# The Fourier branch of a hybrid layer on half of its channel waves, projected as even and odd sums

## What is computed

```python
def _fourier(u):
    b, l, _ = u.shape
    uf = u.astype(jnp.float32).reshape(b, l, FNET_GROUPS, FNET_GROUP_DIM)
    y = jnp.fft.fft2(uf, axes=(1, 3), norm="ortho").real
    return y.reshape(b, l, FNET_WIDTH).astype(u.dtype)
...
    gates = jax.nn.sigmoid(h @ w_gate + b_gate).reshape(b, l, N_BRANCHES, d)
    proj = jnp.einsum("blnw,nwd->blnd", branches, w_branch)
    return jnp.sum(gates * proj, axis=2) @ w_o
```

## Time and profile before

| what | us |
|---|---|
| median of 3 runs | 1163.68 (1163.4 to 1164.49) |
| span of the profiled execution | 1160.8 |
| the rest (launch and end, by the difference from the median) | 2.9 |
| PE busy | 1093.8 (94% of the span) |
| DVE busy | 562.6 (48%) |
| ACT busy | 317.0 (27%) |
| POOL busy | 176.8 (15%) |

### The profile page before, as it was taken

How to read it: one execution, slowest core, us unless ns; L and a number is a source line. 1 busy time by engine, 2 the same in 40 slices (tenths; PEclk the granted TensorE clock), 3 DMA queues, 4 the chain that set the end, 5 groups by cost and what they waited for, 6 DMA issues and landing times.

```text
span 1160.8 us, 16298 instructions
## 1 busy us (share of the span) xinstructions
PE 1093.8 (94%) x5691; PEld 700.4 (60%) x5691; DVE 562.6 (48%) x1011; ACT 317.0 (27%) x539; POOL 176.8 (15%) x255
## 2 busy tenths in 40 slices
PE   6999999989999999999999998899999899988985
PEld 4788888868667777778888777333333233322333
DVE  5776787745676788766564546221112111111114
ACT  4542322243334544342433242100000000000003
POOL 0000110000110323345000100122222122211220
PEclk9999999999999999999999998999999999999999
DMA  9423855720111222223132489989999999999975
GB/s 380 194 97 120 293 177 194 254 91 19 55 56 55 74 73 74 91 85 130 59 109 91 179 368 343 406 352 423 423 424 425 425 426 425 426 427 426 425 321 223
DMA packets 41981, 279.68 MB, mean 241 GB/s; under 512 B 7802, under 2 KB 8186, under 8 KB 30016
## 3 DMA queue, kind: packets, MB, share of 16 engines
q1 hardware_dynamic: 34496, 265.07, 57.3%
q0 software_dynamic: 7424, 13.80, 3.4%
HBM read 274.23 MB, written 13.40 MB: 248 GB/s over the span
## 4 chain that ended last, share of the span: by engine, by line
PE 73%; DMA 14%; DVE 7%; ACT 3%; issue 2%; SPq 0%; DVEq 0%; POOL 0%; ACTq 0%; POOLq 0%
PE psum L701 70%; DMA ering<-in_wb 8%; DMA ering<-in_wa 2%; DMA ada<-in_adaw 2%; DVE ring_lo L1538 1%; PE psum L717 1%; DVE amx L1809 1%; DVE sc L1798 1%; DMA xr<-token_rows,tabt 1%; ACT ring_hi L1235 1%; PE psum L1043 1%; PE psum L741 1%; DMA Hx<-in_xT 1%; DMA gat<-expert_rows 0%; ACT gth L1235 0%
## 5 line engine op out<-in xcount | busy, mean ns | idle before, releaser
L701 PE MATMUL psum<-ering,xs 128*64 128x512 f32 x1056 | 237.0, 599 | 18.7 <-DMA ering<-in_wb 9.1
L701 PE MATMUL psum<-Hhi,ring_hi 128*128 128x512 f32 x472 | 188.3, 399 | 0.1
L701 PE MATMUL psum<-Hlo,ring_hi 128*128 128x512 f32 x472 | 185.3, 393 | 0.2 <-DVE Hlo L1538 0.2
L701 PE MATMUL psum<-Hhi,ring_lo 128*128 128x512 f32 x472 | 183.1, 390 | 0.0
L701 PEld LDWEIGHTS psum<-ering,xs 128*64 128x64 f32 x1056 | 73.2, 137 | 160.9 <-issue 135.1
L1538 DVE TENSOR_TENSOR ring_lo<-ring,ring_hi 128x1024 fp32r<-128x1024 f32 x87 | 107.8, 1239 | 109.7 <-ACT ring_hi L1235 108.6
L1538 DVE TENSOR_TENSOR sg<-sg,psum 128x256 f32<-128x256 f32 x66 | 27.8, 421 | 236.8 <-ACT sg L1235 235.6
L701 PE MATMUL psum<-ering,at 128*64 128x512 f32 x528 | 119.5, 597 | 2.9 <-ACT at L1235 1.6
L1235 ACT ACTIVATE ring_hi<-ring 128x1024 fp32r<-128x1024 f32 x87 | 92.2, 1060 | 74.3 <-DMA ring<-in_stream 41.2
L701 PEld LDWEIGHTS psum<-Hhi,ring_hi 128*128 128x128 f32 x472 | 88.7, 188 | 22.7 <-issue 3.2
L701 PEld LDWEIGHTS psum<-Hhi,ring_lo 128*128 128x128 f32 x472 | 88.5, 188 | 19.7
(11 more groups left out here) (350 smaller groups left out, 1450.7 us busy)
## 6 DMA issues: line engine op xcount, KB each, us to landing
ering<-in_w SPq DMA_DIRECT2D x28, 2048.0 KB, 21.6
ering<-in_wb SPq DMA_DIRECT2D x28, 2048.0 KB, 27.8
ering<-in_wa SPq DMA_DIRECT2D x28, 2048.0 KB, 22.8
ring<-in_stream SPq DMA_DIRECT2D x87, 512.0 KB, 4.3
ada_ring<-in_stream SPq DMA_DIRECT2D x32, 512.0 KB, 3.7
ada<-in_adaw SPq DMA_DIRECT2D x4, 2048.0 KB, 10.8
Am<-decay_rows POOLq DMA_DIRECT2D x8, 512.0 KB, 4.5
gat<-expert_rows SPq DMA_DIRECT2D x4, 1024.0 KB, 8.0
```

Source lines behind the costliest of these rows:

```text
L701: return nc.tensor.matmul(out, lhsT, rhs, start=start, stop=stop)
```

## The change

The transform of a real input is symmetric, so mixer 2 is not expanded any more to 512 waves by 512 positions.

- The channel matrix is 128 x 128: for each group 32 cosines (waves 0 to 31, wave 0 halved) and 32 sines, where the sine of wave 0, which is zero, gives its place to the alternating sum, wave 32. `V` writes one bank (0, 1, 2, 0 in turn) with 4 matmuls of 128 columns. ACT copies each `V` to one buffer that holds all four, and then the alternating columns, three times over, to `alt`, which POOL has cleared behind `("decr",)`.
- `F` are two steps of 4 x 257 and 4 x 255 columns, after all `V`. A new step `FN` transforms the alternating sums (4 matmuls of 258 columns from `alt`). ACT copies the whole of each to `fhi` and `mid`, DVE subtracts for `flo` and the low rows of `mid`.
- The projection folds the weights instead of the data. A `branch` tile of mixer 2 holds the rows of waves 0 to 31 in one half and of waves 0, 63 to 33 in the other. POOL makes their sum and difference (`mixed`, in the tile's `ring_hi` place), ACT copies that to `ring_lo` as the high half, DVE leaves the rest in `ring_hi`. POOL, ACT and DVE do this at the step that `split_at` names.
- `("proj", 2, d)` is first an odd sum over 256 positions (6 matmuls of 256 columns) into bank 0, then an even sum over 258 (6 matmuls of 258 columns, and one more of wave 32 with `mid_w`) into bank 1. ACT copies the odd sum to `odd`; DVE writes sum and difference to `mtmp` (2 operations of 255 columns, one of 2) before it multiplies by the gate.
- A further ring tile and step, `n32`, carry the weight rows of wave 32; ACT and DVE split it into `mid_w` just ahead of `("gate", 2, 0)`.
- The splits of mixer 2's output (4 on ACT, 4 on DVE) are gone. Several semaphores are merged into `step_ready`, `step_exp` and `four_ready`, with the counts in the same order.

```diff
-    t += attention() + [("V", 0), ("V", 1), ("F", 0), ("V", 2), ("F", 1), ("V", 3)] + attention()
-    t += [("F", 2), ("F", 3)] + attention() + attention()
+    t += attention() + [("V", ft) for ft in range(4)] + attention()
+    t += [("F", 0), ("F", 1), ("FN",)] + attention() + attention()
...
+        if n == 2:
+            t += [("n32",)]
...
         elif k == "V":
-            b = 5 - s[1] % 2 * 5
+            b = s[1] % 3
...
         elif k == "F":
-            b = 2 + s[1] % 2 * 5
+            b = 1 + s[1]
+        elif k == "FN":
+            b = 0
...
+        if k == "proj" and s[1] == 2:
+            used[0] = used.get(0, 0) + 1
+            plan["odd", s[2]] = (0, used[0])
...
+                if n == 2:
+
+                    b = claim(pe, ("odd", d))
+                    split_there(x)
+                    if d == 0:
+                        job_read(pe, ("FN",))
+                        pe.wait_ge(mid_w_ready, 1)
+                    for k in range(2):
+                        o = (2 + k) * 256 + d % 2 * P
+                        ins = three(bk(b)[:, 0:256], hi[:, o:o + P], lo[:, o:o + P], fhi[:, k, 256:S], flo[:, k, 256:S], k == 0, k == 1)
+                    ins.then_inc(full[b], 1)
+                    b = claim(pe, s)
+                    for k in range(2):
+                        o = k * 256 + d % 2 * P
+                        three(bk(b)[:, 0:NMID], hi[:, o:o + P], lo[:, o:o + P], fhi[:, k, 0:NMID], flo[:, k, 0:NMID], k == 0, False)
+                    mm(bk(b)[:, 0:NMID], mid_w[:, d * P:d * P + P], mid[:, :], False, True).then_inc(full[b], 1)
+                    continue
...
+            if is_mixed(x):
+                act.wait_ge(mix_ready, 2 * mixed_index[x] + 2)
+                A(hi_place(x), mixed_place(x), ACT.Copy).then_inc(*t(hi_ready))
+                t.settle()
+                return
...
-                A(V[:, ft % 2, :], bk(b, 2), ACT.Copy).then_inc(*t(empty[b], plan[s][1]))
+                got = bk(b).rearrange("p (c a k) -> p c a k", c=NCH, a=2)
+                A(V[:, :, :, ft * HD:ft * HD + HD], got, ACT.Copy).then_inc(*t(act_c))
+
+                got = bk(b).rearrange("p (c a g k) -> p c a g k", c=NCH, a=2, g=2)[:, :, 1, :, 0]
+                A(alt[:, :, :].rearrange("p c (r n) -> p c r n", r=4)[:, :, 0:3, 2 * ft:2 * ft + 2],
+                  got.unsqueeze(2).to_broadcast([P, NCH, 3, 2]), ACT.Copy).then_inc(*t(empty[b], plan[s][1]))
...
+            elif k0 == "proj" and s[1] == 2:
+                b, _n = plan["odd", s[2]]
+                job_full(act, ("odd", s[2]))
+                if s[2]:
+                    job_read(act, ("proj", 2, s[2] - 1))
+                A(odd[:, :], bk(b)[:, 0:256], ACT.Copy).then_inc(*t(empty[b], _n))
...
+                    job_read(v, ("odd", d))
+                    m = NCOS - 1
+                    TT(mtmp[:, 1:m], bk(b)[:, 1:m], odd[:, 1:m], ALU.add).then_inc(*t(dve_c))
+                    TT(mtmp[:, S - 1:m:-1], bk(b)[:, 1:m], odd[:, 1:m], ALU.subtract).then_inc(*t(dve_c))
+                    link(V_.tensor_copy(mtmp[:, 0:NCOS:m], bk(b)[:, 0:NCOS:m]))
...
+            for i in split_at.get(s, []):
+                x = split_tiles[i]
+                if is_mixed(x):
+
+                    arrived(g_, x)
+                    released(g_, hi_before[x])
+                    a, b_ = place(x)[:, 0:S], place(x)[:, S:TILE]
+                    G_.tensor_tensor(mixed_place(x)[:, 0:S], a, b_, ALU.add).then_inc(*t(mix_ready))
+                    G_.tensor_tensor(mixed_place(x)[:, S:TILE], a, b_, ALU.subtract).then_inc(*t(mix_ready))
+                    t.settle()
```

More of the change, by code:

```diff
@@ L158, in tile_of @@
         return (k[0],)
-    if k in ("fu", "q", "cg", "sx", "bg", "zk", "gate", "wo", "macc"):
+    if k in ("fu", "q", "cg", "sx", "bg", "zk", "gate", "wo", "macc", "n32"):
         return s
@@ L166, in is_split, with is_mixed @@
 def is_split(x):
-    return x[0] != "macc"
+    return x[0] not in ("macc", "n32")
+def is_mixed(x):
+    return x[0] == "branch" and x[1] == 2
 def tile_order():
@@ L179, in tile_order @@
             last[x] = s
-    cut = [x for x in order if is_split(x)]
+    cut = [x for x in order if x[0] != "macc"]
     need = dict(first)
@@ L231, in bank_plan @@
             b = 1 + s[1] // 2
-        elif k in ("ynorm", "macc", "zk", "rtk", "dt", "csq", "xa", "seg", "rot", "rope", "seg"):
+        elif k in ("ynorm", "macc", "zk", "rtk", "dt", "csq", "xa", "seg", "rot", "rope", "seg", "n32"):
             continue
@@ L331, in build @@
     ropet = at("ropet", 65536, [P, 4, S])
-    fodd = at("fodd", 57344, [P, 2, 256])
-    V = at("V", 65536, [P, 2, NCH * 256])
+    alt = at("alt", 57344, [P, NCH, P])
+    V = at("V", 65536, [P, NCH, 2, 256])
+    fhi = at("fhi", 110784, [P, 2, S], FR)
+    flo = at("flo", 114880, [P, 2, S], FR)
+    mid = at("mid", 103552, [P, NMID], FR)
+    odd = at("odd", 141504, [P, 256])
+    mid_w = at("mid_w", 142528, [P, D], FR)
+    mixed = at("mixed", RING * TILE * 4, [P, HI_RING, TILE])
     E = at("E", 65536, [P, 2, S])
@@ L509, in build @@
     order, last_use = tile_order()
-    last_on_1 = [s for s in steps[:steps.index(("V", 1))] if s in plan and plan[s][0] == 1][-1]
     raw_index = {}
@@ L516, in build @@
     split_index = {x: i for i, x in enumerate(split_tiles)}
+    mixed_index = {x: i for i, x in enumerate(x for x in split_tiles if is_mixed(x))}
+    wide = [n for n in MIX_ORDER if n != 2]
     spots = {}
@@ L558, in released @@
             eng.wait_ge(macc_ready, s[1] + 1)
+        elif s[0] == "n32":
+            eng.wait_ge(mid_w_ready, 1)
         elif s[0] == "zk" and s[1] < 3:
@@ L967, in _ @@
                     for c in range(NCH):
-                        ins = mm(bk(b)[:, c0:c1], V[:, ft % 2, c * 256 + part * P:c * 256 + part * P + P],
-                                 dftm[:, c, c0:c1], c == 0, c == NCH - 1)
+                        ins = mm(bk(b)[:, c0:c1], V[:, c, part, pair * P:pair * P + P], dftm[:, c, c0:c1], c == 0, c == NCH - 1)
+                ins.then_inc(full[b], 1)
+            elif k0 == "FN":
+                b = claim(pe, s)
+                for c in range(NCH):
+                    ins = mm(bk(b)[:, 0:NMID], alt[:, c, :], dftm[:, c, 0:NMID], c == 0, c == NCH - 1)
                 ins.then_inc(full[b], 1)
@@ L1376, in _ @@
                 job_full(act, s)
-                if s[1] >= 2:
-                    job_read(act, ("F", s[1] - 2))
-                A(fodd[:, s[1] % 2, 0:S - NCOS], bk(b)[:, NCOS:S], ACT.Copy).then_inc(*t(fodd_ready))
+                A(fhi[:, s[1], :], bk(b), ACT.Copy).then_inc(*t(four_ready))
+            elif k0 == "FN":
+                b, _n = plan[s]
+                job_full(act, s)
+                A(mid[:, :], bk(b)[:, 0:NMID], ACT.Copy).then_inc(*t(four_ready))
+            elif k0 == "n32":
+                arrived(act, s)
+                job_full(act, ("proj", MIX_ORDER[MIX_ORDER.index(2) - 1], KD - 1))
+                A(mid_w[:, :], place(s), ACT.Copy).then_inc(*t(four_ready))
             elif k0 == "S":
@@ L1782, in _ @@
                         t.settle()
[L1783 to L1788 removed]
+                v.wait_ge(four_ready, s[1] + 1)
+                TT(flo[:, s[1], :], bk(b), fhi[:, s[1], :].bitcast(F32), ALU.subtract).then_inc(*t(empty[b], plan[s][1]))
+            elif k0 == "FN":
+                v.wait_ge(four_ready, 3)
+                r = slice(32, 64)
+                TT(mid[r, :], bk(b)[r, 0:NMID], mid[r, :].bitcast(F32), ALU.subtract).then_inc(*t(empty[b], plan[s][1]))
+            elif k0 == "n32":
+                v.wait_ge(four_ready, 4)
+                r = slice(64, 96)
+                TT(mid_w[r, :], place(s)[r, :], mid_w[r, :].bitcast(F32), ALU.subtract).then_inc(*t(mid_w_ready))
             elif k0 == "S":
@@ L1881, in _ @@
                    hb(QC[:, Q_SN:Q_SN + 4], P), ALU.mult).then_inc(*t(empty[b], plan[s][1]))
-            elif k0 == "gate" and s[2] == 0:
+            elif k0 == "gate" and s[2] == 0 and s[1] in wide:
                 n = s[1]
@@ L2169, in _ @@
                 G_.dma_start(csd, cst[:, :]).then_inc(decay_in, 16)
+                G_.memset(alt[:, :, :], 0.0).then_inc(*t(padz))
             elif k0 == "st":
@@ L2287, in constants @@
             perm[m - HD // 2, m] = 1.0
-    same = p // HD == f // HD
-    w = 2 * np.pi * ((p % HD) * (f % HD) % HD) / HD
+    half = f % HD // 32 * HD
+    same = p // HD == half // HD
+    w = 2 * np.pi * ((p % HD) * (f % 32) % HD) / HD
+    alternate = np.where(f % 32 == 0, 1.0 - 2.0 * (p % 2), np.sin(w))
+    waves = same * np.where(f < HD, np.where(f % 32 == 0, 0.5, np.cos(w)), alternate)
     prev = np.where(f >= p, 0.0, NEG)
```

109 lines of the change are left out of this document (60 added, 49 removed).

## The result

The changed kernel takes 1183.95 us (median of 4 runs, 1181.39 to 1185.02), the kernel before 1163.54 on the same chip: ratio 1.0182, 95% interval 1.0166 to 1.0197. The direction was forecast, the size was not: 20.4 us slower instead of 9.6, and beyond the upper end of the range, 1180. The profiled run has a span of 1182.0, 21.2 more than before, against 1170.4 in the sum.

A forecast was written before the change was run, and what follows sets the result against it. PE bounds mixer 2 before; after the change it waits on ACT's and POOL's queues. Terms -6.1 + 2.2 + 3.3 + 3.1 + 5.9 - 1.1 = +7.3, with the clock +9.6: 1173.3 us, range 1164 to 1180.

The forecast's parts named there:

- The bound and the sign: Mixer 2: PE bound before; after the change PE waits for ACT's late odd copy, so slower, chance 0.84.
- Step 2: Mixer 2, four blocks of keys: ACT's chain through the second exponential to the odd copy sets the length, 14.95 us.
- Rival 1: PE stays the bound in mixer 2, the odd copy costs nothing, projections save 10.1 us: 1149.7 us, chance 0.08.
- rival 2: Waits exist but are shorter: POOL's fetch in step 3 hidden, no clock fall; 1165.1 us, chance 0.14.
- The transform: From V to the transpose: less PE work, partly offset by F waiting for ACT's V copies; 6.1 us earlier.
- Mixer 3's last step: First mixed tile: POOL waits for the gate, mixes, then ACT rounds; chain on the path, +2.2 us, bounds 0 and 3.4.
- The steps of mixer 2: Gate to gate, waits for odd copy and mix: +3.3, then +3.1 for two, +5.9, and -1.1 for the last four.
- Step 5: Mixer 2, last mix: gate, mix, rounding and split, exponentials, odd copy in a chain of 15.65 us.
- step 1: Mixer 2, has a mix: scores begin at 10.7 instead of 8.9 us after the gate's start; 16.7 us in all.
- The clock: PE's long waits lower the granted clock: one fall in step 3, half of one elsewhere; +2.3 us, ends 0 and 8.
- rival 3: Clock falls in four or five gaps, DVE and POOL hold each other up at some mixes: 1180 us, chance 0.25.
- Costed at nothing: DVE's added operations, the eight ACT copies already in the chain, n32's ring tile (0 to 0.5 us), unchanged mixers 0 and 1.

The follow-up runs named there:

- experiment 1: Changed kernel plus 76 idle matmuls in PE's waits in mixers 3 and 2 (also written `warm`); 1176.3 us, 1.0117 to the kernel before.
- experiment 5: Changed kernel with ACT copying the odd sum between the two exponentials in steps 0 to 5, bank still shared; 1175.14 us, 1.0096 to the kernel before.
- experiment 2: Changed kernel with the new transform but old-form projections (also written `wide`); 1215.07 us, not comparable because the experts get more blocks; mixer 2 108.39.
- no_mix: Changed kernel without POOL's sum and difference of the branch tiles; 1201.91 us, not comparable because the experts get more blocks.
- own_late_warm: Changed kernel with odd sum in bank 2, all four mixes later, 39 idle matmuls in PE's waits; 1161.85 us, 0.9994 to the kernel before.
- early_warm: Changed kernel with early odd copy, all four mixes later, 37 idle matmuls in PE's waits; 1157.73 us, 0.9961 to the kernel before.
- own_bank: Changed kernel with the odd sum in bank 2, computed behind the even sum; 1178.5 us, 1.013 to the kernel before.
- late_one: Changed kernel with only the third branch tile mixed, rounded and split later; 1182.47 us, 1.0166 to the kernel before.

## Why the prediction was right in direction and wrong in size

The steps in us, gate to gate; "full clock" is experiment 1:

| step | before | forecast | full clock | changed |
|---|---|---|---|---|
| 0 | 12.68 | 15.95 | 15.94 | 16.02 |
| 1 | 13.71 | 16.7 | 17.23 | 18.60 |
| 2 | 14.84 | 14.95 | 15.02 | 15.00 |
| 3 | 14.29 | 20.15 | 20.45 | 22.06 |
| 4 | 14.39 | 14.65 | 14.90 | 17.07 |
| 5 | 14.33 | 15.65 | 16.78 | 17.38 |
| 6 and 7 | 24.11 | 21.4 | 21.65 | 23.95 |
| mixer 2 | 108.35 | 119.45 | 121.97 | 130.08 |

- **The bound and the sign**: right. The long waits ahead of gates 1, 2 and 4 are where they were forecast, with `odd` as their releaser, and moving the copy removes them (experiment 5). At gate 6 `odd` doesn't hold PE, and the waits for `sc` and `ytmp` were not in the forecast. Step 2 came out at 15.00 against 14.95 by ACT's chain, but PE's own way is as long: with the copy moved the step still takes 14.86. Rival 1 (PE stays the bound) is excluded, rival 2 (shorter waits) too.
- **The transform** (forecast -6.1): -6.8 by experiment 2, where no fall of the clock lands in `F`. The changed kernel's transpose stands at 269.70, 7.4 earlier than before (of which 0.6 is that the first `V` came earlier), with `F` at 260.98. ACT's `V` copies were costed too high: 0.60 and 0.19 for `alt`, but a pair every 0.72, not 0.86.

```profile
258.06 0.60 ACT L1281 ACTIVATE V<-psum 128x512 f32<-128x512 f32 x1
258.56 0.19 ACT L1281 ACTIVATE alt<-psum 128x24 f32<-128x24 f32 x1
258.78 0.60 ACT L1281 ACTIVATE V<-psum 128x512 f32<-128x512 f32 x1
```
```profile
258.80 1.16 PE L731 MATMUL psum<-CT,uT 128*128 128x128 f32 x8 [2.46 <-ACT alt L1281]
260.98 7.14 PE L731 MATMUL psum<-dftm,V 128*128 128x257 f32 x32 [1.02 <-issue]
...
269.70 0.60 PE L1072 MATMUL psum<-CT,sc 128*128 128x128 f32 x4
```

- **Mixer 3's last step** (+2.2): 15.34 less 13.13, +2.2, partly by luck. POOL's two operations took 2.75 together and not 2.1; but ACT's tanh of 0.7 stands ahead of the rounding in both kernels, and the forecast had ACT round at once. The two slips cancel. Gate (2, 0) as a whole stands 5.1 earlier, forecast 3.9.
- **The steps of mixer 2** (+11.1): +13.6 at the full clock. Step 5 has 1.1 of the missing 2.5, step 1 0.5: the mix takes 1.27 for each operation and up to 1.79, not the 1.04 of the sum.
- **The clock** (+2.3, ends 0 and 8) is the step that failed. It costs 8.1 in mixer 2 and 1.4 more behind it (14.56 less 13.13 at gate (0, 0)), 9.5 together. I priced one fall and a half at 1.4 each; steps 1, 3, 4 and the pair 6 and 7 lost 1.4, 1.6, 2.2 and 2.3 to it (changed less full clock, in the table). The working looked at single long waits, 8 us in step 3, and took a wait of 2.07 as free. The kernel makes waits of 1.1 to 4.1 one behind the other. The clock fell first at gate 1, ahead of step 3; it was low at gate 3 behind waits of 1.27 and 1.09, and in the projection of gate (0, 0) behind one of 1.74. That was rival 3, "everything stretches", at 1180 with a chance of 0.25, and it is what happened, a little stronger.
- **Costed at nothing**: the first gate of mixer 0 was not in the sum. It takes 14.56 instead of 11.40, of which 1.7 is a wait at any clock. PE comes there sooner than POOL's subtractions, so ACT's last `E` and then the splits of mixer 0's output are late against it (the rest, 1.4, is the clock counted above):

```profile
518.90 0.63 ACT L1281 ACTIVATE E<-Am 128x512 f32<-128x512 f32 x1 [2.76 <-POOL Am L2291]
```
```profile
524.74 0.76 PE L731 MATMUL psum<-bhi,ring_hi 128*128 128x512 f32 x1 [1.74 <-ACT ring_hi L1281]
```

So what steps 6 and 7 gain (2.5 at the full clock) is largely given back one step later. The forecast booked the gain and didn't ask who would be late next. That this is the cause is read from the rows. The runs agree: in `wide`, where steps 6 and 7 are as long as before, gate (0, 0) takes 11.40; in `no_mix`, where they are shorter, it takes 13.13 with the same wait of 1.73. No run isolates it.
- **The rest**: from gate (0, 1) to the end 651.26, before 649.84: +1.4, at a granted clock of 0.97 against 0.99. The kernels with the new projections whose clock was full in mixer 2 have 649.2 (`warm`), 649.2 (`own_late_warm`) and 648.6 (`early_warm`), the others 651 to 653. Why the clock of the experts' part should go with that of a part 300 us earlier stays open.

The sum closes: -5.1 + 21.7 + 3.2 + 1.4 = 21.2. The forecast's miss of 11.6 is 7.2 of clock, 2.5 of steps, 1.7 of gate (0, 0) and 1.4 of the rest, less 1.2 at the start. These are differences of two profiles. The start alone differs by up to 3.1 us between kernels that are the same up to there (the gate of mixer 3's last step at 370.76 to 373.89), so the terms of 1 to 2 us are not firm. The clock's 8.1 is borne out by the runs, whose median is 7.7 lower in `warm`.

## What to carry to other kernels

When a change halves an engine's work, the next question is not how much it saves but where the copy that frees its buffer stands in the other engine's queue; moving that one copy between two exponentials was worth 9 us here, moving the mixes behind the fetch 15. A gap of PE costs twice: waits of 1.1 to 4.1 us cost 8 to 10 us more through the clock, so price each place where waits repeat with one fall (1.4 to 2.3 us a step here), and take a forecast of the queues alone only as a lower bound. After removing a wait, look at the clock column before judging the edit: `own_bank` and `late_one` lost a good part of their gain in it.
